# A split matrix kernel's first tiles in another order: gains loaded as rows, VectorE's scales, block A11 first, pair 0's u x z on VectorE

## What is computed

```python
h = rms_norm(x, norm_in[layer])
proj = jnp.einsum('bsd,de->bse', h, w_in[layer])
u_a, v_a, z_a, q_b, k_b, v_b, z_b, gate_a, gate_b = jnp.split(proj, SPLIT_POINTS, axis=-1)
u_a = jax.nn.gelu(u_a)
v_a = rms_norm(jax.nn.gelu(v_a), norm_v[layer])
y_a = chunked_spatial_gating(u_a, v_a, w_s[layer], b_s[layer]) * jax.nn.silu(z_a)
```

## Time and profile before

| | us |
|---|---|
| median of 3 runs | 2602.37 (2602.28 to 2604.38) |
| the profiled execution | 2602.3 |
| its span in the trace | 2600.6 |
| TensorE busy | 2529.3 (97%) |
| VectorE / ScalarE / GpSimd busy | 1536.8 (59%) / 1278.8 (49%) / 1106.0 (43%) |
| mean granted TensorE clock | 0.992 of full |

### The profile page before, as it was taken

How to read it: one execution, slowest core, us unless ns; L and a number is a source line. 1 busy time by engine, 2 the same in 40 slices (tenths; PEclk the granted TensorE clock), 3 DMA queues, 4 the chain that set the end, 5 groups by cost and what they waited for, 6 DMA issues and landing times. The chain is left out here.

```text
span 2600.6 us, 36065 instructions
## 1 busy us (share of the span) xinstructions
PE 2529.3 (97%) x12916; PEld 2139.3 (82%) x12916; DVE 1536.8 (59%) x2033; ACT 1278.8 (49%) x2320; POOL 1106.0 (43%) x908
## 2 busy tenths in 40 slices
PE   6999999999979999999999989999999999999998
PEld 5788888888858888888888768888888888899997
DVE  7545555554575455555555487777777778643333
ACT  6564333434345444443444377677777778411111
POOL 3443232323354544444343377567865667100000
PEclk9999999999989999999999999999999999999999
DMA  3433333333325344455444534334433433633331
GB/s 97 121 97 109 125 101 115 108 104 121 101 67 141 109 137 142 133 157 146 136 138 126 157 95 132 91 107 130 149 94 101 128 111 98 203 130 114 129 114 49
DMA packets 277305, 309.77 MB, mean 119 GB/s; under 512 B 15648, under 2 KB 200992, under 8 KB 277152
## 3 DMA queue, kind: packets, MB, share of 16 engines
q1 hardware_dynamic: 274704, 299.43, 37.7%
q10 hardware_dynamic: 2448, 8.39, 0.8%
HBM read 207.10 MB, written 100.66 MB: 118 GB/s over the span
## 5 line engine op out<-in xcount | busy, mean ns | idle before, releaser
L901 PE MATMUL in_bank<-in_a_hi,in_w_hi 128*128 128x512 f32 x1988 | 785.1, 395 | 27.7 <-ACT in_o L533 10.7
L904 PE MATMUL in_bank<-in_a_hi,in_w_lo 128*128 128x512 f32 x1988 | 776.2, 390 | 0.0
L903 PE MATMUL in_bank<-in_a_lo,in_w_hi 128*128 128x512 f32 x1988 | 776.0, 390 | 0.0
L901 PEld LDWEIGHTS in_bank<-in_a_hi,in_w_hi 128*128 128x128 f32 x1988 | 374.7, 188 | 107.9 <-DVE in_o L773 12.0
L904 PEld LDWEIGHTS in_bank<-in_a_hi,in_w_lo 128*128 128x128 f32 x1988 | 374.4, 188 | 79.2
L903 PEld LDWEIGHTS in_bank<-in_a_lo,in_w_hi 128*128 128x128 f32 x1988 | 375.0, 189 | 75.3
L1425 DVE TENSOR_TENSOR_SCAN att_rest<-att_z_ps,att_rest 128x512 f32<-128x512 f32 (+2 forms) x320 | 358.2, 1120 | 107.8 <-ACT att_z_ps L1389 82.4
L529 ACT ACTIVATE in_w_hi<-in_sums 128x512 fp32r<-128x512 f32 x284 | 178.7, 631 | 487.2 <-PE in_bank L904 331.9
L706 DVE TENSOR_TENSOR in_w_lo<-carried_stage,in_w_hi 128x512 fp32r<-128x512 f32 x213 | 217.1, 1019 | 249.8 <-ACT in_w_hi L529 247.0
L706 DVE TENSOR_TENSOR in_w_lo<-in_sums,in_w_hi 128x512 fp32r<-128x512 f32 x284 | 246.8, 869 | 99.8 <-ACT in_w_hi L529 94.9
L397 POOL TENSOR_TENSOR in_sums<-carried_stage 128x512 f32<-128x512 f32 x71 | 91.8, 1293 | 399.8 <-DMA carried_stage<-in_w_in 399.7
(11 more groups left out here) (183 smaller groups left out, 5002.8 us busy)
## 6 DMA issues: line engine op xcount, KB each, us to landing
carried_stage<-in_w_in SPq DMA_DIRECT2D x144, 512.0 KB, 4.7
carried_wide<-ya_T SPq DMA_DIRECT2D x64, 256.0 KB, 3.2
uz_T<-in_o SPq DMA_DIRECT2D x32, 256.0 KB, 4.6
va_T<-in_o SPq DMA_DIRECT2D x32, 256.0 KB, 3.4
q_T<-in_o SPq DMA_DIRECT2D x32, 256.0 KB, 3.5
k_T<-in_o SPq DMA_DIRECT2D x32, 256.0 KB, 3.6
vb_T<-in_o SPq DMA_DIRECT2D x32, 256.0 KB, 4.1
zb_T<-in_o SPq DMA_DIRECT2D x32, 256.0 KB, 3.6
```

Source lines behind the costliest of these rows:

```text
L901: pe.matmul(bank[:, :], hi, a_hi[:, i, k], start=opens and k == 0, stop=False, skip_group_check=True)
L903: pe.matmul(bank[:, :], hi, a_lo[:, i, k], start=False, stop=False, skip_group_check=True)
L904: mm = pe.matmul(bank[:, :], lo, a_hi[:, i, k], start=False, stop=k == HALF_K - 1, skip_group_check=True)
```

## The change

- **Gains.** They are loaded as 8 rows of 128 (`gain_rows`, in a place of the output buffer), turned by one transpose on TensorE into a PSUM bank and copied to `gain` by VectorE.
- **Scales.** Tiles 2 and 3 are scaled by VectorE, not by ScalarE.
- **Order of halves.** `TURNS` lists the half tiles: both halves of tiles 0 and 1, then the lower halves of 2 and 3, then their upper halves, then the rest. Turns, keeps and waits follow it. ScalarE's rounding of A11 waits only until the lower halves of tiles 0 to 3 are kept. TensorE runs the plain block P1, then turns tile 4, then runs P2.
- **VectorE's list** is changed to go with it: the rest of A11 and A21 before tile 4 is kept.
- **u x z of pair 0** is taken from GpSimd and put on VectorE behind the weight rests of P3 and P5. SyncE's stores and VectorE's own waits name the new semaphores.
- **U2 of pair 1** comes right behind `n4`; the split of T1 (the rest of P5's right operand) and the rest of P4's weights follow it inside `pair(1)`.

The diff (the new semaphores left out; context shortened):

```diff
@@ -166,6 +166,7 @@
         p1, u2, u3, o11, o22 = (o[:, i] for i in range(5))
+        gain_rows = o[0:KT, 0, 0:P]
         o12, o21 = u2, u3
...
@@ -225,8 +228,17 @@
         FREE_2, FREE_1 = 2, 1
-        SCALED_BY_DVE = [0, 1, 4, 6]
+        SCALED_BY_DVE = [0, 1, 2, 3, 4, 6]
         SCALED_BY_ACT = [u for u in range(TILES) if u not in SCALED_BY_DVE]
+        TURNS = [(u, half) for u in range(2) for half in range(2)]
+        TURNS += [(u, half) for half in range(2) for u in range(2, HALF_K)]
+        TURNS += [(u, half) for u in range(HALF_K, TILES) for half in range(2)]
+        def turn_of(u, half):
+            return TURNS.index((u, half)) if u < TILES else 2 * u + half

@@ -253,7 +265,7 @@
                 elif u >= len(x_bufs):
-                    sp.wait_ge(turned, 2 * (b + 1))
+                    sp.wait_ge(turned, turn_of(b, 1) + 1)
                 sp.dma_start(x_bufs[b], x_t[u]).then_inc(x_loaded[b], 16)
@@ -345,9 +357,15 @@
                         load_w(n + 2)
-                    sp.wait_ge(uz1_done, uz_before(n) + 1)
+                    if n:
+                        sp.wait_ge(uz1_done, uz_before(n))
+                    else:
+                        sp.wait_ge(first_uz1, 1)
                     sp.dma_start(s["uz_T"][rows, t1], o11).then_inc(stored11, 16)
-                    sp.wait_ge(uz2_done, uz_before(n) + 1)
+                    if n:
+                        sp.wait_ge(uz2_done, uz_before(n))
+                    else:
+                        sp.wait_ge(first_uz2, 1)
                     sp.dma_start(s["uz_T"][rows, t2], o22).then_inc(stored22, 16)
@@ -365,8 +383,7 @@
             load_x(1)
-            with nc.allow_non_contiguous_dma(reason="1024 gains, one to a partition"):
-                sp.dma_start(gain[:, :], norm_in[0].rearrange("(k p) -> p k", p=P)).then_inc(gain_loaded, 16)
+            sp.dma_start(gain_rows, norm_in[0].rearrange("(k p) -> k p", p=P)).then_inc(gain_loaded, 16)
             load_x(2)
@@ -441,7 +458,7 @@
                     pool.tensor_tensor(h12, h22, h12, ALU.subtract).then_inc(t3_done, 1)
-                if is_uz(n):
+                if is_uz(n) and n:
                     pool.wait_ge(c11_done, FREE_2 + n + 1)
@@ -502,7 +519,7 @@
                 if i == P1 or i == P2 or i == P3:
-                    act.wait_ge(h_done, 2 * TILES * (g + 1) if g or i == P3 else TILES)
+                    act.wait_ge(h_done, 2 * TILES * (g + 1) if g or i == P3 else turn_of(HALF_K - 1, i == P2) + 1)
                 elif i == P6:
@@ -604,9 +621,7 @@
             first_squares(2)
-            scale(2)
             first_squares(3)
-            scale(3)
             round_plain_w(P1)
@@ -622,6 +637,7 @@
             round_a(P3, 0)
+            act.wait_ge(turned, turn_of(4, 1) + 1)
             act.wait_ge(plain, 1)
@@ -666,7 +682,7 @@
                 ks = slice(half * HALF_K, (half + 1) * HALF_K)
-                dve.wait_ge(turned, 2 * u + half + 1)
+                dve.wait_ge(turned, turn_of(u, half) + 1)
                 dve.tensor_tensor(h_T[:, ks, at:at + P],
@@ -766,12 +782,16 @@
                 dve.wait_ge(p1_done, n + 1)
-                if before_uz:
-                    dve.wait_ge(uz2_done, uz_before(n))
+                if n == 1:
+                    dve.wait_ge(first_uz2, 1)
+                elif before_uz:
+                    dve.wait_ge(uz2_done, uz_before(n) - 1)
                 else:
...
                 if n == 1:
+                    rest_a(P5, 0)
+                    rest_w(P4, 1)
                     rest_a(P4, 0)
@@ -779,8 +799,10 @@
                 dve.wait_ge(prod[P7], n + 1)
-                if before_uz:
-                    dve.wait_ge(uz1_done, uz_before(n))
+                if n == 1:
+                    dve.wait_ge(first_uz1, 1)
+                elif before_uz:
+                    dve.wait_ge(uz1_done, uz_before(n) - 1)
                 else:
@@ -823,24 +845,28 @@
             mean(1)
-            dve.wait_ge(gain_loaded, 16)
+            dve.wait_ge(gain_turned, 1)
+            dve.tensor_copy(gain[:, :], banks[3][:, 0:KT]).then_inc(gain_kept, 1)
             scale(0)
+            scale(1)
             mean(2)
-            keep_both(0)
-            scale(1)
+            dve.wait_ge(gain_kept, 1)
+            keep(0, 0)
             mean(3)
-            keep_both(1)
-            keep_both(2)
-            keep_both(3)
+            keep(0, 1)
+            scale(2)
+            scale(3)
+            for u, half in TURNS[2:TILES]:
+                keep(u, half)
             rest_plain_w(P1)
             mean(4)
+            rest_a(P1, 0)
             scale(4)
-            rest_a(P1, 0)
             rest_plain_w(P2)
+            rest_a(P2, 0)
+            mean(5)
+            mean(6)
             keep_both(4)
-            mean(5)
-            rest_a(P2, 0)
-            mean(6)
             scale(6)
@@ -864,13 +890,15 @@
             rest_w(P5, 1)
+            dve.wait_ge(c11_done, FREE_2 + 1)
+            dve.wait_ge(f21_done, 1)
+            dve.tensor_tensor(o11, o11, o21, ALU.mult).then_inc(first_uz1, 1)
+            dve.wait_ge(f22_done, 1)
+            dve.wait_ge(f12_done, 1)
+            dve.tensor_tensor(o22, o12, o22, ALU.mult).then_inc(first_uz2, 1)
+            dve.sem_inc(u3_done, 1)
+            dve.sem_inc(c12_done, 1)
             n4()
-            rest_a(P5, 0)
-            rest_w(P4, 1)
-            dve.wait_ge(f21_done, 1)
-            dve.sem_inc(u3_done, 1)
-            dve.wait_ge(f12_done, 1)
-            dve.sem_inc(c12_done, 1)
             for n in range(1, LAST):
@@ -973,11 +1001,14 @@

-            def first_turn(u):
+            def first_turn(u, half):
                 if u >= 2:
-                    pe.wait_ge(h_done, 2 * u - 2)
-                for half in range(2):
-                    turn(u, half)
+                    pe.wait_ge(h_done, turn_of(u - 2, half) + 1)
+                turn(u, half)
+            def turn_gain():
+                pe.wait_ge(gain_loaded, 16)
+                pe.transpose(banks[3][:, 0:KT], gain_rows, ident[0:KT, 0:KT]).then_inc(gain_turned, 1)

@@ -1004,11 +1035,19 @@
                 pe.sem_inc(prod[i], 1)
-            for u in range(5):
-                first_turn(u)
-            plain_11_21(bank_a[0], P1, P2)
-            for u in range(5, TILES):
-                first_turn(u)
+            turn_gain()
+            for u, half in TURNS[:TILES]:
+                first_turn(u, half)
+            pe.wait_ge(w_ready[P1], 1)
+            pe.wait_ge(a_ready[P1], 1)
+            plain_block(bank_a[0], P1, P1, True, False)
+            for half in range(2):
+                first_turn(HALF_K, half)
+            pe.wait_ge(w_ready[P2], 1)
+            pe.wait_ge(a_ready[P2], 1)
+            plain_block(bank_a[0], P2, P2, False, True).then_inc(plain, 1)
+            for u, half in TURNS[TILES + 2:]:
+                first_turn(u, half)
             plain_11_21(bank_b[0], P5, P4)
```

More of the change, by code:

```diff
@@ L203, in norm_and_project @@
         first_squared, first_scaled = sc.sem("first_squared"), sc.sem("first_scaled")
+        gain_turned, gain_kept = sc.sem("gain_turned"), sc.sem("gain_kept")
+        first_uz1, first_uz2 = sc.sem("first_uz1"), sc.sem("first_uz2")
         a12_hi_done, a12_ready, plain = sc.sem("a12_hi_done"), sc.sem("a12_ready"), sc.sem("plain")
```

## The result

The changed kernel takes **2607.73 us** (median, 2605.33 to 2610.75), the one before, run beside it, 2602.62 us (2601.55 to 2605.42). The ratio is 1.0018, with a 95% interval of 1.0012 to 1.0025: 5.1 us slower by the medians, just inside the 0.2% up to which no change was spoken of, while the interval reaches past it. 2605.0 was forecast, 2.7 us slower, in a range up to 2608.2: the median lies 0.5 us inside it, and the loss is nearly twice the likeliest one. The profiled executions are 2606.33 and 2602.3 us (spans 2604.6 and 2600.6), so the trace has 4.0 us to account for; that of the changed kernel is 1.4 us faster than its median. The granted clock is 0.989 on the mean, against 0.992.

A forecast was written before the change was run, and what follows sets the result against it. The start of P3 of pair 1 and TensorE's speed from there were taken as the bound: 2602.3 + 1.8 (later load) - 1.6 (front gain) + 0.3 (stores) + 2.2 (clock) = 2605.0 us, range 2600.8 to 2608.2.

The forecast's parts named there:

- What bounds the kernel: When P3 of pair 1 starts (79.26 us before) and how fast TensorE runs from there.
- C: Rival: pair 2's weights aren't the last wait, P3 of pair 1 starts at 70.3 us; 2593.3 us; chance 0.05.
- The front: First tiles and blocks: block P1 starts at 20.0 us, 2.5 us earlier; gain 1.6 us at 59.4 us.
- rival A: First block P1 at full clock: gain 4.1 us, time 2602.5 us; chance 0.2.
- Rival B: Tile 4's turn between blocks P1 and P2 keeps the clock low: 2608.5 us, slower by 0.24%; chance 0.1.
- D: Rival: loads not faster, nothing gained at the start; gain 0 to 0.5 us, 2606.1 to 2606.6 us; chance 0.15.
- U2 ahead: Pair 1: n4 ends just when P6 is done, U2 is ready at 61.9 us, P7 starts there instead of 67.68.
- G: Gain from the first tiles and blocks at 59.4 us: 1.6 us, bounds 0 and 4.1.
- The first term, + 1.8: Pair 2's load comes 1.8 us later: 1.2 us of u x z and 0.6 of U2 go ahead on VectorE.
- the - 1.6: Gain from the first tiles and blocks, taken off the start of P3 of pair 1: 1.6 us.
- Stores beside the load: Both stores of pair 0's u x z make pair 2's load land 0.3 us later, bounds 0 and 0.9.
- The clock behind P3: Pair 1: slow matmuls follow the idle piece before P3 and cost 2.2 us, bounds 1.5 and 3.3.

The follow-up runs named there:

- gain_rows_only: The kernel before with only the gains loaded as 8 rows, turned and copied: 2602.47 us, ratio 0.9998.
- front_only: The kernel before with gains as rows, scales, order of halves and blocks; u x z on GpSimd and U2 as before: 2601.26 us, ratio 0.9992.
- back_only: The kernel before with only u x z of pair 0 on VectorE and U2 of pair 1 ahead of the splits: 2609.1 us, ratio 1.0025.
- fill_before_p3: The changed kernel with 36 repeated matmuls on TensorE ahead of P3 of pair 1: 2605.76 us, ratio 1.0012.
- before_p4_early: The kernel before with the rounding and rest of P4's weights of pair 1 moved ahead of N4: 2600.6 us, ratio 0.9995.
- fill_both: The changed kernel with repeated matmuls in pair 1, 14 ahead of P1 and 36 ahead of P3: 2603.3 us, ratio 1.0003.
- u2_behind_split: The changed kernel with U2 of pair 1 back behind the splits, u x z staying on VectorE: 2605.47 us, ratio 1.0013.
- p4_weights_early: The changed kernel with P4's weights of pair 1 split ahead of the u x z products: 2600.84 us, ratio 0.9995.

## Why the prediction was right, and where it wasn't

**What bounds the kernel: right.** The start of P3 and the clock behind it carry the loss; the sum released by L817 stands ahead of P3 with 8.74 us of wait (9.5 forecast), and the long wait before P7 could go without any gain. C is refuted. Two of the signs named for this were missed: the load was to be issued near 64.7 and went out at 66.63, and P7 was to start near 62 and started at 63.86.

**The front: right at the block, too small behind it.** The block P1 starts at 19.97 (20.0 forecast). The gains alone gave 0.8 us of that by `gain_rows_only`. The trace of before was read as 1.0 us for tile 2; it is 0.56 us earlier in `gain_rows_only` and 0.47 in the changed kernel. The Trainium skill's rate, "DMA: Bandwidth & Descriptors", section Measured, made 0.67 by estimate, which is nearer. The turns of tiles 5 and 6 begin at 27.79 and not at 29.0, because the matmuls get short from 22.67 us on: the low stretch covered half of the block P1 only. This is part of rival A. Rival B is refuted: tile 4's eight transposes between the blocks took 1.04 us, and P2 behind them ran at full speed. The window 23 to 30 us has a granted clock of 1.00. The Trainium skill, "TensorE: Matmul & The Clock Gate", Part 4, would have transpose mode not count as busy; here the turn, with the clock up already, didn't lower it, which a turn of 1.04 us tests only weakly. Longer runs of transposes don't agree with each other: from 7.86 to 16.2 us the changed kernel's stayed long (16 in 3.67 us, then 4 in 0.97 to 1.11), while in `front_only`, with no other matmuls ahead of them, they got short at 12.28 (4 in 0.60 to 0.66). D, no front gain, is refuted at this place: VectorE was 2.14 us earlier at 57 us (1.6 forecast). The time of `front_only` can't be told from that of the kernel before.

**U2 ahead: the step that failed.** The prediction let P6 end at 62.72 - G and so U2 wait for nobody. TensorE didn't keep its lead: it reached P1 of pair 1 at 51.20 instead of 53.34, but had stood 3.69 us instead of 2.6, and P1 then ran at the low clock. P1 to P2 took 6.15 us instead of 3.65, and P2 started 0.36 us later than before. P7 started at 63.86, not at 62, and VectorE waited 2.39 us with the staging buffer's last reader queued behind. The first term, + 1.8 for the later load, was right by itself, and + 2.39 is missing from the sum; the - 1.6, in truth - 2.14 on VectorE, was eaten by it.

That U2 waits for TensorE hangs on the new front: in `back_only` VectorE makes it right behind N4 without a wait. How long it waits differs. `fill_before_p3` has the same instructions as the changed kernel up to this place, and there U2 waited 1.40 us. The 3.69 us ahead of P1 of pair 1 have no releaser in the profile and stand in this one trace; in the ten others without filling there the wait is 2.56 to 2.61 us. In P1 behind it seven or eight matmuls are long in eight of the ten, two of which have the first tiles in the old order (`before_p4_early`, `gain_rows_only`), and none in the kernel before and in `back_only`; the changed kernel's trace has twelve. So the low clock at P1 isn't made by the new front alone, and why it came here and not in the kernel before stays open.

**Stores beside the load: not seen here.** + 0.3 was taken; 5.81 us from issue to landing against 6.08 is - 0.3, just under the lower bound of 0. With the same two stores behind the load other traces have 5.75 (`fill_both`), 5.92 (`back_only`), 6.12 (`fill_before_p3`) and 7.17 us (`u2_behind_split`), so a single trace can't settle this term.

**The clock behind P3: right in place, too large for this trace.** P3 starts with a matmul of 0.80 us, and the window 77 to 86 us has a clock of 0.62. 2.2 us were forecast, from 1.5 to 3.3. The rows give 1.48 us here, 1.3 in `u2_behind_split` and 2.3 in `back_only`, and 0 where the wait is filled.

**By the sum.** At P3 + 0.5 us was forecast and + 1.83 measured, for the clock + 2.2 and + 1.48. Two errors of opposite sign left the sum at + 3.3 where + 2.7 was forecast: that it came out so near was luck in part. Behind the first turn of the steady loop the trace has + 2.6 us at attention and + 4.0 at the end. From that turn to attention the traces differ by up to 1.4 us (1403.1 us in the changed kernel, 1403.9 in the kernel before, 1404.5 in `back_only`), and 1.4 us are added in attention and merge; both kernels run the same instructions there. In the windows above, the clock from 1490 to 1515 us is 0.73 in the changed kernel, from 2230 to 2245 0.77; in the kernel before they have 0.80 and 0.89. `front_only` and `gain_rows_only` have 0.73 and 0.77 too, and they aren't slower. So the longer low clock there isn't tied to one part of the change. Whether it belongs to the 5.1 us of the medians, or only to these executions, stays open. The prediction had no term for it, and the median stayed inside the range without one.

## What to carry to other kernels

On an engine that works its list in order, ask of each instruction that is put ahead what it waits for and who stands behind it: U2 was wanted early, but its wait (2.4 us in the trace) went to the last reader of a single staging buffer, and that buffer's load set the start of P3. A long wait is worth its length only if no later one takes it over, so find the last one first, and after each edit look for the same fault one step later. Follow a gain at the start through every wait up to that last one: an engine that arrives earlier may only stand longer, and work at the low clock behind that can take the gain back.

## What the hardware showed that was not expected

- **VectorE and GpSimd get longer side by side.** In `p4_weights_early` GpSimd's subtraction took 3.16 instead of 1.53 us beside VectorE's rests, which took 5.58 instead of 4.5 us for two. The 1.1 us more on VectorE are about one sum of GpSimd (1.26), as if the one waited for the other's running instruction; no run tests this. GpSimd's product took 9.87 us in the kernel before, while VectorE ran without a gap, where the next took 1.26; in `front_only`, `before_p4_early` and `gain_rows_only` it took 9.87 again.
- **Low stretches differ between stages and executions.** The first block P1 took 4.2 us here, behind an idle of 3.74 us, and 5.26 before, where 0.91 us and a turn stood ahead of it. Two stages that no edit touches had mean clocks of 0.80 and 0.89 in two kernels (the one before, `fill_both`) and of 0.73 and 0.77 in three others. A few microseconds on a kernel of 2600 can't be put down to one place without the rows of the others.
- **Filling idle time with repeated matmuls gave 4.4 us on one kernel and nothing on another** (2607.73 to 2603.3; 2597.81 to 2599.4).
- **The granted clock at the start of a trace says little.** In the kernel before it reads 1.00 from 8 to 10 us, where eight transposes took 1.97 us; from 30.58 us on, also at 1.00, sixteen took 1.91. There the lengths tell more than the column.
